# A hybrid decoder step on one core: two narrow input units packed into one of 97 columns, with the mixer's steps, taps and GpSimd work reordered

## The reference

```python
h = x + 0.5 * post1(SwiGLU1(pre1(x)))
u = preM(h); P = u @ w_in                       # one combined input projection
[A | B | C | D] = Conformer conv | GLA | short gated conv | forgetting attention
h = h + postM(concat(A, B, C, D) @ w_out)
h = h + 0.5 * post2(SwiGLU2(pre2(h)))
```

## Time and profile before

| what | value |
|---|---|
| time before, median of 3 runs | 1066.25 us (1065.76 to 1067.06) |
| profiled execution, its own time | 1065.38 us |
| its span, first to last instruction | 1063.6 us |
| granted TensorE clock, mean | 0.999 of full speed |
| PE busy | 1052.0 us, 99% |
| DVE busy | 687.2 us, 65% |
| ACT busy | 570.8 us, 54% |
| POOL busy | 278.4 us, 26% |

### The profile page before, as it was taken

One profiled execution on the slowest core, in us unless ns is written; L12 is line 12 of the kernel. 1 busy time (PEld: TensorE's weight loads), 2 busy tenths in 40 slices (PEclk: granted clock), 3 DMA queues, 4 the chain that ended last, 5 costly groups with the idle time before them and its releaser, 6 DMA issues. The chain is left out here.

```text
span 1063.6 us, 24197 instructions
## 1 busy us (share of the span) xinstructions
PE 1052.0 (99%) x8978; PEld 1023.3 (96%) x8978; DVE 687.2 (65%) x1032; ACT 570.8 (54%) x970; POOL 278.4 (26%) x344
## 2 busy tenths in 40 slices
PE   8999999999999999999999999999999999999997
PEld 8999999998999999999999999999989999999997
DVE  5666644599977666654476666446999766666442
ACT  6544454576477644454464444546665765444542
POOL 4222220204505222220142222103054233222202
PEclk9999999999999999999999999999999999999999
DMA  7656567452735665556646556763536456565561
GB/s 278 216 178 185 174 218 243 128 160 88 231 100 182 205 191 178 178 171 187 184 131 200 180 176 189 226 202 121 174 101 210 122 175 217 178 189 174 173 187 45
DMA packets 62882, 187.42 MB, mean 176 GB/s; under 512 B 9162, under 2 KB 18514, under 8 KB 62674
## 3 DMA queue, kind: packets, MB, share of 16 engines
q1 hardware_dynamic: 62802, 186.31, 56.1%
HBM read 182.90 MB, written 3.38 MB: 175 GB/s over the span
## 5 line engine op out<-in xcount | busy, mean ns | idle before, releaser
L318 DVE TENSOR_TENSOR w_lo<-raw,w_hi 128x1024 fp32r<-128x1024 f32 (+1 forms) x316 | 412.3, 1310 | 321.9 <-ACT w_hi L308 321.7
L308 ACT ACTIVATE w_hi<-raw 128x1024 fp32r<-128x1024 f32 x336 | 344.3, 1030 | 239.1 <-PE ub L352 170.7
L350 PE MATMUL ub<-hg_hi,w_hi 128*128 128x264 f32 x976 | 281.2, 288 | 0.7 <-issue 0.7
L351 PE MATMUL ub<-hg_lo,w_hi 128*128 128x264 f32 x976 | 276.6, 283 | 0.0
L352 PE MATMUL ub<-hg_hi,w_lo 128*128 128x264 f32 x976 | 276.3, 283 | 0.0
L350 PE MATMUL ub<-act_hi,w_hi 128*128 128x264 f32 x704 | 200.5, 285 | 0.0
L352 PE MATMUL ub<-act_hi,w_lo 128*128 128x264 f32 x704 | 200.0, 284 | 0.0
L351 PE MATMUL ub<-act_lo,w_hi 128*128 128x264 f32 x704 | 199.1, 283 | 0.0
L350 PE MATMUL quad<-hg_hi,w_hi 128*128 128x264 f32 x696 | 198.6, 285 | 0.0
L351 PE MATMUL quad<-hg_lo,w_hi 128*128 128x264 f32 x696 | 197.2, 283 | 0.0
L352 PE MATMUL quad<-hg_hi,w_lo 128*128 128x264 f32 x696 | 197.1, 283 | 0.0
(11 more groups left out here) (262 smaller groups left out, 1283.6 us busy)
## 6 DMA issues: line engine op xcount, KB each, us to landing
raw<-in_w_gu SPq DMA_DIRECT2D x176, 512.0 KB, 4.0
raw<-in_w_dn SPq DMA_DIRECT2D x64, 512.0 KB, 3.9
raw<-in_w_in SPq DMA_DIRECT2D x44, 512.0 KB, 3.8
raw<-in_w_dn SPq DMA_DIRECT2D x32, 384.0 KB, 3.4
raw<-in_w_out SPq DMA_DIRECT2D x16, 512.0 KB, 3.8
pages<-in_cache_k SPq DMA_DIRECT2D x32, 128.0 KB, 3.4
pages<-in_cache_v SPq DMA_DIRECT2D x32, 128.0 KB, 3.2
con<-in_con SPq DMA_DIRECT2D x1, 1192.0 KB
```

What stands on the lines that cost most here:

```text
L308: eng.activation(w_hi[:, slot, 0:w], raw[:, slot, 0:w], ACT.Copy).then_inc(*sig("hi_ready", reps))
L318: eng.tensor_tensor(w_lo[:, slot, 0:w], raw[:, slot, 0:w], w_hi[:, slot, 0:w].bitcast(F32), ALU.subtract)\
L350: eng.matmul(out, a_hi, x_hi[:, k0 + k, :], start=(first and k == 0), stop=False)
L351: eng.matmul(out, a_hi, x_lo[:, k0 + k, :], start=False, stop=False)
```

## The change

The 16 low-rank columns and the 4 forget gates share one unit of 97 columns: gates in columns 0, 32, 64 and 96, low-rank columns in 1 to 16. The matmul with `wa2` reads 17 rows, the first against a row of `wa2` that holds zeros. The phase `in` has 23 units, numbered one lower each from `BQ` on; its 24th place is left empty, the last real unit counts for two, and slot 3 of the ring has one turn fewer in each layer (`empty_turns`). All `proj=` counts drop by one. Steps 0 to 18 stay with the unit of their number; the unit 19 carries steps 19 and 20 (on PE `mix` of both after it); later units carry the step one higher. Taps start in step 11, right behind their inputs: taps 0 to 2 are summed in `ymix` in SBUF, tap 3 reads that sum and writes PSUM. POOL's first half unit waits for the six instructions of taps 0 to 2, and its unit 21 for the products of `a_dec`.

```diff
-ALR, FG, BQ, BK, AG, BG, AV, BV, DQ, DKK, DVV, CC, CX, CB = 0, 1, 2, 3, 4, 6, 8, 10, 12, 14, 16, 18, 19, 22
-IN_WIDTH = [16, 97] + [P] * 22
+ALR, FG, BQ, BK, AG, BG, AV, BV, DQ, DKK, DVV, CC, CX, CB = 0, 0, 1, 2, 3, 5, 7, 9, 11, 13, 15, 17, 18, 21
+IN_UNITS = 23
 FGW = 97
+ALR_ROWS = 17
+IN_WIDTH = [FGW] + [P] * (IN_UNITS - 1)
...
-POOLED = tuple(range(14, 24))
-TAPS = {12: (0, 4), 13: (4, 10), 15: (10, 16), 16: (16, 22), 17: (22, 26), 18: (26, 28), 19: (28, 31)}
+POOLED = tuple(range(14, 23))
+TAPS = {11: (0, 3), 12: (3, 7), 13: (7, 11), 15: (11, 17), 16: (17, 23), 17: (23, 27), 18: (27, 29), 19: (29, 31)}
+EARLY_TAPS = 3
...
+        def parts_of(s):
+
+            return (s,) if s <= 18 else (19, 20) if s == 19 else (s + 1,)
...
-                for n in range(GROUP, 24):
+                for n in range(GROUP, IN_UNITS):
...
-                    mix(l, n)
-                pe.wait_ge(*at(l, "proj", 24))
+                    for part in parts_of(n):
+                        mix(l, part)
+                pe.wait_ge(*at(l, "proj", IN_UNITS))
...
                 if n == 12:
 
-                    after(l, proj=12)
+                    after(l, proj=11)
                     for j in range(2):
                         for b in range(TD):
                             act.activation(v_diag[:, j * TD + b, :], const("lvm", CH), ACT.Copy, scale=proj[:, BV + j, TP + b:TP + b + 1])\
...
-                        y, x, w = taps_sum[:, c * TP:(c + 1) * TP], a_pad[:, c, t:t + TP], par[:, PAR["acw"] + c * TAPS_A + t:PAR["acw"] + c * TAPS_A + t + 1]
+                        x, w = a_pad[:, c, t:t + TP], par[:, PAR["acw"] + c * TAPS_A + t:PAR["acw"] + c * TAPS_A + t + 1]
+                        early, late = ymix[:, YA + c, 0:TP], taps_sum[:, c * TP:(c + 1) * TP]
                         if t == 0:
-                            after(l, b_msk=7)
-                            dve.tensor_scalar(y, x, w, par[:, PAR["acb"] + c:PAR["acb"] + c + 1], ALU.mult, ALU.add).then_inc(*sig("a_tap"))
+                            after(l, a_in=1)
+                            dve.tensor_scalar(early, x, w, par[:, PAR["acb"] + c:PAR["acb"] + c + 1], ALU.mult, ALU.add).then_inc(*sig("a_tap"))
                         else:
                             after(l, a_tap=k - 1)
-                            out = ymix[:, YA + c, 0:TP] if t == TAPS_A - 1 else y
-                            dve.scalar_tensor_tensor(out, x, w, y, ALU.mult, ALU.add).then_inc(*sig("a_tap"))
+                            if t == EARLY_TAPS:
+                                after(l, b_msk=7)
+                            out = early if t < EARLY_TAPS or t == TAPS_A - 1 else late
+                            dve.scalar_tensor_tensor(out, x, w, early if t <= EARLY_TAPS else late, ALU.mult, ALU.add).then_inc(*sig("a_tap"))
...
                     if s >= 1:
                         evacuate(s - 1)
-                    mix(l, s)
+                    for part in parts_of(s):
+                        mix(l, part)
                     if s > GROUP:
                         rest_unit(dve, lead, reps)
-                    behind(l, s)
+                    for part in parts_of(s):
+                        behind(l, part)
                 steps(dve, "in", l, inp, 24)
-                evacuate(23)
-                mix(l, 24)
...
                 clear_pads(l)
+                after(l, a_tap=2 * EARLY_TAPS)
                 for n in POOLED:
+                    if n == 21:
+                        after(l, a_dp=2)
                     rest_halves(pool, l, n)
```

More of the change, by code:

```diff
@@ L231, in tile_of, with no_unit, counted, empty_turns @@
             return tiles[:, n, :] if isinstance(n, int) else tiles[:, bass.ds(n, 1), :].rearrange("p a c -> p (a c)")
+        def no_unit(phase, idx):
+            return phase == "in" and idx == IN_UNITS
+        def counted(phase, idx):
+            return 2 if phase == "in" and idx == IN_UNITS - 1 else 1
+        def empty_turns(layer, phase, slot):
+            if slot != IN_UNITS % RING:
+                return 0
+            return layer + (phase in ("out", "gu1", "dn1"))
+        def parts_of(s):
+            return (s,) if s <= 18 else (19, 20) if s == 19 else (s + 1,)
         def steps(eng, phase, l, body, pattern=4, peel_first=False):
@@ L259, in turn @@
                         slot=(s + LEAD) % RING, number=l * UNITS + first + i * pattern + s + LEAD,
-                        turn=l * (UNITS // RING) + first // RING + i * (pattern // RING) + (s + LEAD) // RING))
+                        turn=l * (UNITS // RING) + first // RING + i * (pattern // RING) + (s + LEAD) // RING - empty_turns(row, ph, (s + LEAD) % RING)))
             if peel_first:
@@ L278, in turn_before @@
             if lead["phase"] == "out" and lead["index"] < RING:
-                return "in", lead["index"] + PHASES["in"][1] - RING
+                back = lead["index"] + PHASES["in"][1] - RING
+                return "in", back if back < IN_UNITS else back - RING
             return lead["phase"], lead["index"] - RING
@@ L307, in round_unit @@
             eng.wait_ge(S["unit_done"], lead["number"] + 1)
-            eng.activation(w_hi[:, slot, 0:w], raw[:, slot, 0:w], ACT.Copy).then_inc(*sig("hi_ready", reps))
+            eng.activation(w_hi[:, slot, 0:w], raw[:, slot, 0:w], ACT.Copy).then_inc(*sig("hi_ready", reps, counted(lead["phase"], lead["index"])))
         def rest_unit(eng, lead, reps):
@@ L331, in fourth_unit @@
             first = PHASES[phase][0]
-            return dict(index=3, phase=phase, layer=l, width=COLS, slot=3, number=l * UNITS + first + 3, turn=l * (UNITS // RING) + first // RING)
+            return dict(index=3, phase=phase, layer=l, width=COLS, slot=3, number=l * UNITS + first + 3,
+                        turn=l * (UNITS // RING) + first // RING - empty_turns(l, phase, 3))
         def final(l, q):
@@ L340, in first_unit, with multiply_unit @@
             return dict(index=s, phase="gu0", layer=0, weights=ins["w_gu0"], row=s, width=COLS, slot=s, number=s, turn=0)
-        def multiply_unit(eng, out, slot, x_hi, x_lo, tiles, k0, first, last, reps, ready=None, inside=None):
+        def multiply_unit(eng, out, slot, x_hi, x_lo, tiles, k0, first, last, reps, ready=None, inside=None, count=1):
             for k in range(tiles):
@@ L723, in mix @@
                     after(l, proj=1)
-                    pe.matmul(mb[2][:, 0:NT], par[0:16, PAR["wa2"]:PAR["wa2"] + P], proj[0:16, ALR, :], start=True, stop=True).then_inc(*sig("b_z"))
+                    pe.matmul(mb[2][:, 0:NT], par[0:ALR_ROWS, PAR["wa2"]:PAR["wa2"] + P], proj[0:ALR_ROWS, ALR, :], start=True, stop=True).then_inc(*sig("b_z"))
                 if 5 <= n <= 11:
@@ L742, in mix @@
                     decode_back(l)
-                    after(l, proj=18, d_sm=4)
+                    after(l, proj=17, d_sm=4)
                     transposes(mb[2], proj[:, DVV:DVV + 2, :], "d_vT")
@@ L1166, in level_keys @@
             def level_keys(l, i):
-                after(l, b_E=i, proj=4, b_qs=1)
+                after(l, b_E=i, proj=3, b_qs=1)
                 if i >= 3:
@@ L1251, in mix @@
                 if n == 16:
-                    after(l, proj=16)
+                    after(l, proj=15)
                     dve.wait_ge(zeroed, 1)
@@ L1361, in short_gate @@
                 y = ymix[:, YC + c, :]
-                after(l, proj=23 + c)
+                after(l, proj=22 + c)
                 dve.tensor_tensor(y, y, proj[:, CB + c, :], ALU.mult).then_inc(*sig(("c_y", "c_y1")[c]))
@@ L1605 @@
     win = np.zeros((L, 24, P, COLS), f32)
-    for n in range(24):
+    for n in range(IN_UNITS):
         m = IN_WIDTH[n]
```

49 lines of the change are left out of this document (25 added, 24 removed).

## The result

The changed kernel takes 1074.74 us, the median of 4 runs (1074.47 to 1077.09); the kernel before took 1066.15 us beside it, the median of 4 (1065.76 to 1067.06). The ratio is 1.0078, with a 95% interval of 1.0066 to 1.0090: 8.6 us slower, where 4.1 were forecast. The forecast had the direction, but the time lies 2.7 us outside the range. The profiled execution took 1074.73 us, 9.35 more than that of before, in a span of 1072.9 us and at a mean granted clock of 0.994 instead of 0.999.

A forecast was written before the change was run, and what follows sets the result against it. PE, busy 99% of the span, was taken to bound the kernel, with DVE nearly full in the mixer. Lateness of 2.05 us into `out` per mixer, 4.1 in both, gave 1070.3 us, range 1064.0 to 1072.0.

The forecast's parts named there:

- Matmuls: In each mixer, the removed unit's 24 matmuls save PE 2.96 us, 5.9 in both, if nothing else is late.
- PE's wait before L679: In each mixer, PE's 0.85 us wait goes, since ACT starts about 2.1 us sooner.
- The rows of DVE: In the mixer, GpSimd's half units delay DVE: tap 3's pair 1.4 us, `qe` 1.0, `pm` 0 to 1.2.
- The two ends on `pm`: Delay of `pm` in step 16: 0 by the earlier profile row, 1.2 us by the skill's rule; 1.2 taken.
- Where lateness decides: At step 17's evacuation, DVE is 1.1 to 2.3 us late; `dstat` ends about 278.8, PE's L628 starts 1.87 us later.
- To the last tap: From L1375 at 287.3, 7.4 us of DVE work: last tap at 294.7, `conv_sum` at 294.8 against 294.58 before.
- to `out`: Copy, rounding and split follow `fox_outputs` serially, 2.94 us: third unit of `out` at 311.8, 2.05 us later per mixer.
- Nothing after the mixer changes: Behind the late third unit of `out`, the rest keeps its time, so no further cost is added.
- the sum 2 x 2.05: Lateness at `out` in both mixers totals 4.1 us, giving 1070.35 us on the median of 1066.25.
- The rivals: Tap 3 not held, 1064.5 us, chance 0.17; one half late, 1066.6, 0.13; whole gain, 1058.6, 0.04; more collisions, 1072.8, 0.06.
- whole gain: Rival for both mixers: if DVE's order did not matter, 7.6 us saved, 1058.6 us; chance 0.04.

The follow-up runs named there:

- the run where GpSimd was held: GpSimd's unit 18 held until the two `pm` products are done, on the kernel with early rounding and holds for tap 3 and unit 20: 1061.21 us.
- the last experiment: One tap moved from step 19 to step 16, on the kernel with early rounding and GpSimd's four holds, the `state` one included: 1058.37 us, ratio 0.9921.
- the early rounding: Changed kernel with ACT's rounding of the third unit of `out` ahead of step 23, and DVE's split of it moved ahead: 1069.47 us.
- the packing alone: Changed kernel's packed unit, 23 units and paired steps, with the taps and GpSimd's free start of the kernel before: 1077.97 us, ratio 1.0109.
- both holds: Changed kernel with GpSimd held until tap 3 is done, and its unit 20 until the scan and `dstat` of step 17 are done: 1069.22 us.
- the second group of runs: The second four follow-up kernels, measured beside the unchanged kernel before, which took 1066.76 us there, 1065.59 to 1068.07 in twelve runs.
- the run before it: GpSimd's unit 16 held until the `state` products and sum are done, added to early rounding and holds for tap 3, unit 20 and `pm`: 1060.05 us.

## Why the prediction was right in its steps and wrong in its sum

- *Matmuls, and PE's wait before L679.* Right: 48 fewer, and no wait there.
- *The rows of DVE.* Right within 0.3 us: tap 3's pair lost 1.2 us (forecast 1.4), `qe` 0.9 (1.0), `pm` 1.1 (1.2). The two ends on `pm` differed, and the rule won here: the row of before said 0, and the rule does not explain why `pm` passed there. By that rule (the Trainium skill, SBUF — State Buffer, "Who interferes with whom") the two-input instruction waits for the whole GpSimd one; the trace agrees, with 1.57 us against 0.38 in the run where GpSimd was held.
- *Where lateness decides.* Right in place and size: the evacuation of step 17 without idle time, `dstat` through at 278.74, `gla_norm` at 279.96. Wrong in attribution: tap 3 was not what made step 17 late. What was lost there could be taken away without any gain (1075.31 us), because the halves then met `state`; and the run that freed `state` as well, last, gained only 1.2 us. The scan's collision with unit 20 and `pm`'s with units 18 and 19 set it: freeing them moved `dstat` by 1.1 and 1.0 us.
- *To the last tap, and to `out`.* Right: 294.58 and 311.60, by the serial chain of copy, rounding and split. The lateness is 1.84 us in the first mixer for a forecast of 2.05, and 0.20 of the 1.84 come from the program's start; a mixer adds 1.64.
- *"Nothing after the mixer changes", and with it the sum 2 x 2.05.* This is the step that failed. PE's waits of 2.0 and 2.7 us were priced at their own length; at three of the four the granted clock fell to half, and each fall cost another 1.5 us. Of the 9.35 us of the profiled execution, 4.6 are the three falls (what the run with dummies in the same waits gave back), 3.3 the lateness that the forecast put at 4.1, 1.0 the rests at the start of the second mixer, which it put at nothing, 0.2 the program's start, and 0.3 stay unassigned. With PE kept busy in the waits the kernel takes 1070.16 us, where the forecast was 1070.3. That these agree so well is luck: the lateness was put 0.8 us too high, the rests and the start, 1.2 us, were not in the sum, and it stood on a median that is 0.87 us above the profiled execution.
- *The rivals.* None named the clock. The "whole gain" of 1058.6 was put at what it would be if DVE's order did not matter; the last experiment reaches 1058.37 by ordering GpSimd and DVE so that it hardly does. That the two numbers agree is in part chance: this run has also lost PE's waits of 0.3 us before `out`, and it keeps about 1.0 us for the rests in the second mixer.

What stays open: which wait draws a fall, and why one fall lasts twice as long as the others. Four kernels have two waits of 2.7 us before `gla_norm` (the changed one, the early rounding, tap 3 freed, the packing alone), and in each profiled execution exactly one of the two had a fall, in the first mixer or in the second. Of the two waits of 2.0 us in `out` it was both in the changed kernel and in the packing alone, one with tap 3 freed, and none with both holds. The kernels with such waits scatter by 2.6 to 3.2 us, those without by 0.3 to 1.4, but scatter alone is no sign of falls: the kernel before, whose mixers have no such wait, scatters by 2.5 us beside the second group of runs, and its mean clock (0.997 to 1.000) does not follow its time. The last kernel's profiled execution, 1059.78 us where the other four took 1058.36 to 1058.59, has a fall at the program's start: a wait of 2.2 us for nothing that the profile names, and a mean clock of 0.79 from 12 to 20 us. In the run before it the same wait is 2.1 us, and no fall follows. None of the runs tells what decides in a single case. Why the two `hg_lo` were late in the second mixer alone was not tried either; it costs about 1.0 us in every run but the packing alone.

## What to carry to other kernels

Price a wait of the matmul engine twice: its own length, and a stretch at half clock beside it, which cost about 1.5 us here for a wait of 2.0 to 2.7, and 2.75 once. It may come in one execution and not in the next, and that belongs in the range. Two engines that lock each other out keep their collisions when one of them is shifted: look for what the shifted work meets next, and hold it by the instructions that it must not meet, each by name, as long as its consumer has time. And after a unit is taken out of a pipeline, read the last step before the next phase: what had a step of its own may now stand behind the phase's last result.

## What the runs showed of the hardware

- The granted clock fell from 2.4 to 1.2 GHz at PE's waits of 2.0 and 2.7 us, between 0.8 us before such a wait ended and 1.4 us after it, and not at all of them; in the mixers of these profiled executions never at those of 1.7 us or less. A fall cost about 1.5 us (9.13 us from the third unit's start to `y_sq`, 7.58 with the clock kept up), and 2.75 in the one that lasted twice as long. The Trainium skill, TensorE: Matmul & The Clock Gate, Part 1, has a gate that falls when PE is idle; that added matmuls make the kernel faster (1074.74 to 1070.16 us) agrees with it.
- An instruction of the form SCALAR_TENSOR_TENSOR with both tensors in SBUF was held up by GpSimd like a TENSOR_TENSOR (the tap 3 pair 1.98 us, and 0.89 without GpSimd; three `state` instructions 3.33 and 1.53), and so was a scan (1.61 and 0.68). With one tensor in PSUM, the same form ran at 0.4 us each while GpSimd was at its halves.
- Two like instructions in a row do not always both wait: `pm` passed in 0.45 us in the kernel before and took 1.57 in the changed one, both with GpSimd at work.
